# A two-block transformer kernel on one core: the first filter tap of a short convolution, the order of weight splits and four DMA issues change engines or places

## The reference, cut to what matters

```python
# even layer: bias of each head by distance, projections, compression of keys and values
hp @ w_in                      # q, k, v and the rest, one product
silu(blocks @ w1) @ w2         # blocks of 32 rows, for keys and for values
table[:, rel_bucket(dist)]     # added to the scores of 16 heads
# mixer: projection, causal depthwise convolution with 4 taps, silu
proj = h @ w_in
xbc = silu(causal_depthwise_conv(xbc, conv_w, conv_b))   # 1536 channels, out[t] = b + sum_w conv_w[w] * u[t - 3 + w]
```

## Time and profile before

| what | value |
|---|---|
| median of 3 runs | 1286.62 us (1284.84 to 1290.71) |
| the profiled execution's own time | 1286.62 us |
| its span, first to last instruction | 1284.8 us |
| TensorE busy | 95% |
| VectorE, ScalarE, GpSimd busy | 65%, 51%, 18% |
| mean granted TensorE clock | 0.982 |

### The profile page before, as it was taken

The page is one execution under the profiler, slowest core; times in us unless marked ns, Lnnn a source line. Parts: engine busy times, 40 slices in busy tenths (PEclk is TensorE's granted clock), DMA queues, the critical chain, the costliest instruction groups (busy, mean ns, idle before and its releaser), DMA issues.

```text
span 1284.8 us, 19110 instructions
## 1 busy us (share of the span) xinstructions
PE 1223.2 (95%) x7700; PEld 1058.4 (82%) x7700; DVE 839.2 (65%) x1308; ACT 656.0 (51%) x1076; POOL 230.9 (18%) x284
## 2 busy tenths in 40 slices
PE   7897899999999889999999999999999889999996
PEld 6785588888888568888888889999996579888996
DVE  6955586665586467666657776467766756766743
ACT  6425566644333556664446555446635444655531
POOL 4003431110000332121112221000005201112101
PEclk9999999999999999999999999999999879999999
DMA  7790155564454324555544554543440024455461
GB/s 275 269 200 14 54 197 171 190 222 174 163 197 155 141 99 173 188 196 194 184 182 162 196 198 153 197 175 141 162 185 1 1 77 162 164 196 175 155 206 56
DMA packets 34088, 205.56 MB, mean 160 GB/s; under 512 B 3776, under 2 KB 6352, under 8 KB 13776
## 3 DMA queue, kind: packets, MB, share of 16 engines
q1 hardware_dynamic: 30704, 200.47, 44.0%
q10 hardware_dynamic: 3296, 3.87, 1.6%
HBM read 202.87 MB, written 1.46 MB: 159 GB/s over the span
## 4 chain that ended last, share of the span: by engine, by line
PE 79%; DVE 14%; ACT 3%; POOL 1%; issue 1%; DMA 0%; POOLq 0%; ACTq 0%; DVEq 0%
PE ps L660 35%; PE ps L665 23%; PE ps L663 5%; PE ps L664 5%; DVE wl L602 4%; PE ps L684 1%; PE ps L686 1%; PE ps L685 1%; DVE tf L2173 1%; POOL pb L992 1%; PE ps L907 1%; PE ps L973 1%; ACT wh L573 1%; DVE y L1960 1%; DVE xb L738 1%
## 5 line engine op out<-in xcount | busy, mean ns | idle before, releaser
L602 DVE TENSOR_TENSOR wl<-raw,wh 128x2048 fp32r<-128x2048 f32 (+4 forms) x196 | 421.2, 2154 | 150.6 <-ACT wh L573 150.4
L660 PE MATMUL ps<-xb,wh 128*128 128x512 f32 x1424 | 502.3, 398 | 4.4 <-DVE wl L602 3.9
L665 PE MATMUL ps<-xb,wl 128*128 128x256 f32 x1696 | 476.2, 281 | 0.0
L573 ACT ACTIVATE wh<-raw 128x2048 fp32r<-128x2048 f32 (+4 forms) x196 | 348.6, 1781 | 157.9 <-PE ps L665 123.6
L660 PEld LDWEIGHTS ps<-xb,wh 128*128 128x128 f32 x1424 | 267.4, 188 | 71.1 <-issue 5.6
L665 PEld LDWEIGHTS ps<-xb,wl 128*128 128x128 f32 x1696 | 321.5, 190 | 0.0
L665 PE MATMUL ps<-ab,wl 128*128 128x256 f32 x1088 | 307.2, 282 | 0.0
L660 PE MATMUL ps<-ab,wh 128*128 128x512 f32 x640 | 226.8, 399 | 0.8 <-DVE ab L1002 0.8
L665 PEld LDWEIGHTS ps<-ab,wl 128*128 128x128 f32 x1088 | 207.0, 190 | 0.0
L660 PEld LDWEIGHTS ps<-ab,wh 128*128 128x128 f32 x640 | 120.2, 188 | 31.7 <-DVE ab L1002 1.4
L857 DVE TENSOR_TENSOR tf<-ps,tf 128x256 f32<-128x256 f32 x148 | 61.9, 421 | 119.3 <-ACT tf L852 119.3
(11 more groups left out here) (326 smaller groups left out, 1372.1 us busy)
## 6 DMA issues: line engine op xcount, KB each, us to landing
raw<-wstream SPq DMA_DIRECT2D x156, 1024.0 KB, 4.8
raw<-wstream SPq DMA_DIRECT2D x32, 704.0 KB, 4.1
raw<-wstream SPq DMA_DIRECT2D x8, 768.0 KB, 4.2
e_bt<-scratch ACTq DMA_DIRECT2D x16, 128.0 KB, 9.7
o_bt<-scratch SPq DMA_DIRECT2D x2, 1024.0 KB, 10.2
raw<-wstream SPq DMA_DIRECT2D x2, 560.0 KB, 10.1
raw<-wstream SPq DMA_DIRECT2D x4, 256.0 KB, 6.4
h<-xt ACTq DMA_DIRECT2D x4, 256.0 KB, 7.5
```

The lines of the kernel that those rows point to most:

```text
L573: e.g.activation(WH[i % HLN][:, 0:w], RAW[i % RAWN][:, 0:w], ACT.Copy).then_inc(S["hi"], 1)
L602: e.g.tensor_tensor(WL[q][:, 0:w], RAW[i % RAWN][:, 0:w], f32(WH[q][:, 0:w]), ALU.subtract).then_inc(S["lo"], 1)
L660: e.g.matmul(PS[b][:, :].rearrange("p (a t) -> p a t", a=2), wh[:, sl], x2[:, :, cs], start=start, stop=k == p.nk - 1, skip_group_check=pair)
L665: ins = e.g.matmul(o, wl[:, sl], xh[:, cs], start=False, stop=k == p.nk - 1, skip_group_check=pair)
```

## The change

1. The convolution's tap 1 moves from VectorE to GpSimd: for each of 12 tiles one multiply into the upper half of `tf` and one add to ScalarE's result. VectorE keeps taps 2 and 3, and waits for GpSimd. The lags go: VectorE does pair p-1 behind evicting pair p, ScalarE applies the silu of pair p-1 ahead of tap 0 of pair p.
2. `behind_norm`, `next_low`, `tight` and the early low part of u4 go: low parts follow the plain rule of `dve_gemm`, and so does the high part of u5; `mz` is taken with `behind` 1 instead of 0.
3. The low parts of `cmpk` and `cmpv` ahead of and inside `km` go, and follow the plain rule.
4. The scratch write and both spreads go from ScalarE's queue to SyncE's, between the weight fetches; the load of `vecs` goes from the head of ScalarE's queue to the second place of SyncE's.

```diff
-        def dve_gemm(e, p, behind, after=None, drain=None, ahead=2, first=None, between=None, tight=0):
+        def dve_gemm(e, p, behind, after=None, drain=None, ahead=2, first=None, between=None):
...
-                        lo_to(e, i + 2 - tight)
+                        lo_to(e, i + 2)
...
                 e.g.dma_start(RAW[0][:, s], w0[:, s]).then_inc(S[f"q{i}"], 16)
+                if i == 0:
+                    e.g.dma_start(V[:, :], vdram).then_inc(S["d_v"], 16)
...
         def act_begin(e):
-            e.g.dma_start(V[:, :], vdram).then_inc(S["d_v"], 16)
...
             sp_gemm(e, G["km"])
-            for name in ("cmpk", "cmpv", "qn", "ks", "ev0"):
+            e.wait_ge(S["row"], 1)
+            row = TMP[1][0:16, 0:384]
+            e.g.dma_start(bass.AP(scratch.tensor, 0, [[16 * 385, 16], [385, 16], [1, 384]]),
+                          bass.AP(row.tensor, row.offset, [list(row.ap[0]), [0, 16], [1, 384]])).then_inc(S["d_scr"], 16)
+            for name in ("cmpk", "cmpv", "qn"):
                 sp_gemm(e, G[name])
+            spread_bias(e, 1)
+            sp_gemm(e, G["ks"])
+            sp_gemm(e, G["ev0"])
+            spread_bias(e, 0)
...
-            lo_to(e, G["cmpk"].first + 1)
-            dve_gemm(e, G["km"], 1, drain=dve_to(G["km"], e_km, 0), between=lambda e, c: lo_to(e, G["cmpv"].first))
+            dve_gemm(e, G["km"], 1, drain=dve_to(G["km"], e_km, 0))
...
+            def drain_u(e, pair):
+                if pair:
+                    silu_u(pair - 1)
+                e.wait(G["mu"].out[pair])
+                e.wait_ge(S["zero"], 3)
+                for f in (2 * pair, 2 * pair + 1):
+                    e.g.activation(TF[f % 4][:, 0:T], uv[:, f, 0:T], ACT.Identity, scale=v_("convw", 4 * f, 1),
+                                   bias=v_("convb", f, 1)).then_inc(S["cva"], 1)
...
-            act_gemm(e, G["mu"], after=behind_norm, drain=drain_u)
+            act_gemm(e, G["mu"], after=act_finish(5, 1e-6), drain=drain_u)
...
         def pool_mixer(e):
+            for pair in range(6):
+                for f in (2 * pair, 2 * pair + 1):
+                    c, d = TF[f % 4][:, 0:T], TF[f % 4][:, T:2 * T]
+                    e.wait(G["mu"].out[pair])
+                    e.wait_ge(S["zero"], 3)
+                    if f >= 4:
+                        e.wait_ge(S["cts"], f - 4 + 1)
+                    e.link(e.g.tensor_scalar(d, uv[:, f, 1:1 + T], v_("convw", 4 * f + 1, 1), 0.0, ALU.mult, ALU.add))
+                    e.settle()
+                    e.wait_ge(S["cva"], f + 1)
+                    e.g.tensor_tensor(c, c, d, ALU.add).then_inc(S["cvp"], 1)
...
-                    e.wait_ge(S["cva"], f + 1)
-                    for w in (1, 2, 3):
+                    e.wait_ge(S["cvp"], f + 1)
+                    for w in (2, 3):
...
-                if pair == 0:
-                    lo_to(e, p.first + 4)
-                if pair >= 2:
-                    taps_u(pair - 2)
+                if pair:
+                    taps_u(pair - 1)
...
-                if pair < 2:
-                    taps_u(4 + pair)
-
-            def next_low(e, c):
-                if c > 2:
-                    lo_to(e, G["mu"].first + c + 2)
-
-            dve_gemm(e, G["mu"], 1, after=dve_finish(5, 1e-6, then=scaled(32.0 ** -0.5)), drain=drain_u, between=next_low,
-                     tight=1)
-            dve_gemm(e, G["mz"], 0, drain=drain_z)
+                if pair == 0:
+                    taps_u(5)
+
+            dve_gemm(e, G["mu"], 1, after=dve_finish(5, 1e-6, then=scaled(32.0 ** -0.5)), drain=drain_u)
+            dve_gemm(e, G["mz"], 1, drain=drain_z)
```

More of the change, by code:

```diff
@@ L371, in stream_no @@
     return 1 + at // 4 if c == 0 else 5 + at // 8 if c == 1 else 5 + c
-SEMS = ("er ct0 ct1 gated iv ptd rl eps psa psb pss pr ysq ysum acc adt ah al blk blkh blkl bt0 bt1 const cq cts cum cva cvd cz d_c d_out d_scr d_v ea "
+SEMS = ("er ct0 ct1 gated iv ptd rl eps psa psb pss pr ysq ysum acc adt ah al blk blkh blkl bt0 bt1 const cq cts cum cva cvd cvp cz d_c d_out d_scr d_v ea "
         "ev_act ev_dve rel low ex fah fal gemm gp gq gs gz h_down0 h_down1 h_eo h_oo hi lam_a lam_d lf lo mh ml mx na "
@@ L1142, in act_even @@
                 e.g.activation(e_blkh[:, sl], blk[i][:, 0:480], ACT.Copy).then_inc(S["blkh"], 1)
[L1143 to L1146, removed]
             act_gemm(e, G["km"])
@@ L1155, in act_even @@
             act_gemm(e, G["qn"])
-            spread_bias(e, 1)
             act_gemm(e, G["ks"])
-            spread_bias(e, 0)
             act_gemm(e, G["ev0"], drain=act_toks(G["ev0"], e_v, 0, 0))
@@ L2053, in silu_u @@
                     e.g.activation(uv[:, f, 3:259], TF[f % 4][:, 0:T], ACT.Silu).then_inc(S["cts"], 1)
[L2055 to L2071, removed]
+            def drain_u(e, pair):
[6 more added lines that the diff above has]
+                                   bias=v_("convb", f, 1)).then_inc(S["cva"], 1)
             def drain_z(e, pair):
-                if pair < 3:
-                    drain_u(e, 6 + pair)
+                if pair == 0:
+                    silu_u(5)
                 zs = m_zs[:, pair * 512:pair * 512 + 512]
@@ L2170, in taps_u @@
                     c = TF[f % 4][:, 0:T]
-                    e.wait_ge(S["cva"], f + 1)
-                    for w in (1, 2, 3):
+                    e.wait_ge(S["cvp"], f + 1)
+                    for w in (2, 3):
                         ins = e.g.scalar_tensor_tensor(out=c, in0=uv[:, f, w:w + T], scalar=v_("convw", 4 * f + w, 1), in1=c,
                                                        op0=ALU.mult, op1=ALU.add)
-                        if w < 3:
+                        if w == 2:
                             e.link(ins)
```

## The result

| | before | changed |
|---|---|---|
| median of 7 runs each | 1287.83 us (1284.84 to 1290.71) | 1299.47 us (1293.99 to 1306.98) |
| the profiled execution's own time | 1286.62 us | 1302.14 us |
| its span | 1284.8 us | 1300.3 us |
| mean granted TensorE clock | 0.982 | 0.977 |

The ratio is 1.0113, with a 95% interval of 1.0090 to 1.0137; that is 11.6 to 17.6 us. The medians lie 11.6 us apart, the two profiled executions 15.5 us. With the others on record there are 24 executions of the changed kernel: one disturbed one (1513.77 us at a mean granted clock of 0.743) is left out, and the median of the other 23 is 1302.14 us. The forecast was +8.0 us, 1294.6 us, so its side was right and its size too small. The median of the seven lies just inside the stated range of 1287.5 to 1300 us, the profiled execution and the median of the 23 lie above it.

What follows compares the result with a forecast made beforehand. The prediction took TensorE, busy 95% of the span, as the bound, so gaps ahead of matmuls count. Mixer 6.4, even-layer splits 0.6, spread 1.0 and vectors 0 sum to +8.0 us: 1294.6 us, 8-in-10 range 1287.5 to 1300.

Steps and rivals of the forecast that it cites:

- stall ahead of u5: Mixer's start: u5's low part comes behind three pairs' taps, so TensorE starts u5 5.9 us late.
- clock behind it: Mixer, behind u5's stall: TensorE runs at 1.2 GHz instead of 2.4 for a while, +1.6 us.
- given back at q0 and q1: Mixer: the delay fills TensorE's idle 0.83 us ahead of q1 and about 0.3 ahead of q0, -1.1 us.
- even-layer splits and scratch write: Even layer's start: reordered low parts make chunk 9 0.6 us late; the scratch write delays chunk 7's fetch 1.1 us, costing nothing.
- the spread: Even layer: half the bias ahead of chunk 13's fetch delays the drain of ks some 2 us; +1.0, from 0 to +4.
- vectors: Kernel's start: vecs on SyncE's queue is the same bytes ahead of the same instruction; 0, from -0.7 to +0.8 us.
- The ring: Mixer's convolution: each pair passes VectorE's taps, ScalarE's silu and tap 0, GpSimd's multiply and add; 4.21 us a pair.
- rival (c): Mixer: GpSimd is held by VectorE's taps, 0.95 us more for each of three pairs, +2.9, 1297.5 us; chance 0.13.
- rival (d): Even layer: chunk 13 so late that TensorE waits 4 us ahead of ev0; +5 instead of +1, 1298.6 us; chance 0.12.
- a sign of being wrong: Even layer: the prediction called itself wrong if ev0 started over 4 us late; it expected 1 to 2 us.
- (a): Mixer: tap 0, silu and GpSimd always keep ahead of VectorE; mixer +0.3 us, whole +1.9, 1288.5 us; chance 0.15.
- (b): Mixer: VectorE's lighter round removes TensorE's idle times ahead of u5, q0 and q1; 1284.5 us; chance 0.05.

Runs made afterwards that it cites:

- e1: Kernel before with only the even layer's part: vectors' load, scratch write and spreads on SyncE's queue, low parts by the plain rule; 1293.07 us, ratio 1.0047.
- e12: Changed kernel with 52 extra matmuls, whose results nobody reads, ahead of u5; 1299.33 us, ratio 1.0102 to before.
- e10: Kernel before with the whole new mixer (short lags, new split order), but tap 1 on VectorE; 1296.03 us in one run.
- e4: Kernel before with only both spreads of the bias moved to SyncE's queue; 1290.70 us, ratio 1.0026.
- e13: As e4, but chunk 13's fetch goes ahead of the first half of the spread on SyncE's queue; 1285.31 us in one run.
- e5: Kernel before with only the scratch write moved, ahead of chunk 7's fetch on SyncE's queue; 1295.22 us in one run.
- e7: Kernel before with e5's scratch write and e6's low parts together; 1288.79 us in one run.
- e6: Kernel before with only the low parts of cmpk and cmpv around km put on the plain rule; 1285.31 us in one run.
- e11: Kernel before with only tap 1 moved to GpSimd, old lags and split order kept; 1288.66 us, ratio 0.9992.
- e3: Kernel before with only the load of vecs moved to the second place of SyncE's queue; ratio 0.9994.
- e9: Kernel before with only the new convolution in the mixer (GpSimd's tap, short lags), old split order kept; 1303.58 us in one run.
- e15: Kernel before with tap 1 on GpSimd at the old lags and u4's low part ahead of the norm; 1289.34 us, ratio 1.0003.

## Why the prediction was wrong, by its own steps

| term of the sum | forecast, us | measured, us |
|---|---|---|
| stall ahead of u5 | 5.9 | 7.1 |
| clock behind it | 1.6 | 1.95 |
| given back at q0 and q1 | -1.1 | -0.7 |
| the mixer | +6.4 | +8.35 |
| even-layer splits and scratch write | 0.6 + 0 | 2.6 (same code in e1, e12: 1.1, 1.0) |
| the spread | 1.0 | 2.4 + 1.5 behind it (e1, e12: 5.0, 4.9) |
| vectors | 0 | 1.35 (e1, e12: 0.95, 1.2) |
| sum | +8.0 | +16.2 |

Between `ev0` and u4 0.3 us are given back, which makes the 15.9 at q1; 15.5 are left at the end.

**The mixer: the mechanism held, its size was short.** The ring gates, GpSimd and ScalarE stand between VectorE's pieces, there is one stall, its clock loss follows and q1 gives 1.0 us back. The ring was put at 4.21 us and takes 4.6. In it the term that was mis-sized is the taps'. The forecast took them at 0.48 us each and let the ring close over the second tile's; in the chain it closes over all four, 0.70 + 1.48 + 0.50 us with a hop. The source views of the taps, changed kernel and kernel before (ns, min/median/max):

```profile
L2177 DVE SCALAR_TENSOR_TENSOR tf<-m_u,vecs,tf x24: 474/655/846, 892.0 to 922.1; 128x256 f32<-128x256 f32 x24
```

```profile
L2173 DVE SCALAR_TENSOR_TENSOR tf<-m_u,vecs,tf x36: 473/485/486, 886.2 to 917.0; 128x256 f32<-128x256 f32 x36
```

and of GpSimd's add in the changed kernel:

```profile
L2140 POOL TENSOR_TENSOR tf<-tf x12: 725/774/1708, 891.2 to 920.1; 128x256 f32<-128x256 f32 x12
```

Four taps take 2.7 us for a pair now, where the forecast had 1.9. In e10, with the same lags and without GpSimd, a tap takes 484 ns in the median and 486 at most, so it is GpSimd beside them that makes them longer. GpSimd's add keeps its 0.77 us beside them and has 1.7 only beside a low part. So rival (c) was right that sharing costs time and wrong about who pays: not GpSimd, held for 0.95 us in each of three pairs, but VectorE. The ring grew by 0.4 us, which is 0.7 over the two rings behind pair 0; pair 0's own round took 0.6 more. So u5 is 1.2 us later than forecast, not 2.9. The rule of the Trainium skill, "GPSIMD Engine Reference", section "Specifications", that GpSimd contends with VectorE instructions with two SBUF inputs, agrees with these rows; the prediction held against it and looked only at GpSimd's side. The same group shows VectorE's: two of L738 in 1.43 us beside GpSimd, 0.72 each, and a tap of that kind takes 0.48.

**The spread: the step that failed most.** The prediction put chunk 13 near 73 us, its low part's end near 77 and the drain of `ks` some 2 us later. On before's clock (3.97 us taken off) the copy starts at 74.0, the low part ends at 78.2 and the drain comes 3.5 us later. It then priced the drain's delay at 1.0, half of it, by the small products of the compression. They hide only 1.2 us: TensorE waits 2.2 us (+2.4 on the lateness), and the stretch at the low clock behind it takes 1.5 more (1.7 in e4, 2.5 in e1 and e12); 4.0 us alone in e4. That is rival (d), which had 0.12, and `ev0` starts 6.4 us late, past the 4 us that the prediction named as a sign of being wrong. The row that decides was there: the earlier trace rows has 10.2 us for a megabyte in rows of 1 KB, the half that now goes first. "The same bytes cross the same engines now" was the wrong reason against (d). Before, chunk 13 is fetched 4 us ahead of that traffic, and it is chunk 15 that takes 12.3 us to land, with time to spare; in the changed kernel chunk 13 is fetched behind it. e13 moves only that and the loss is gone.

The Trainium skill, "DMA: Bandwidth & Descriptors", section "Issuing engines are not separate DMA queues", says that DMAs run on the same 16 engines and interleave, whichever engine starts them. These traces agree: e13 issues the same spreads from SyncE without loss, and the 12.3 us of chunk 15 in before come with the spreads on ScalarE's queue.

**The scratch write: "nothing is lost" was wrong.** The fetch of chunk 7 goes out at 38.39 as forecast, but the copy can only start at 48.16, 9.8 us on, against the 4.8 of the earlier trace rows; the 384 KB ahead of it cost it 5 us of landing on top of the 1.1 us of issue. By itself this costs 3.0 us (e5), with the new splits 0.8 to 1.1 us (e7, e1, e12), and 2.6 in the changed kernel's own trace. The splits' own +0.6 was near (e6, +0.4), though the prediction's terms 43.9 + 4.8 + 1.9 give 50.6 and not the 51.1 that it wrote; but the idle times ahead of chunks 7, 8 and 9, which were to take up their delay, were now used up by the late landings.

**The vectors: outside the bounds.** The bytes are the same, but `vecs` lands at 8.6 us in the second place of SyncE's queue, where the prediction had 7.26 and at most +0.8. The first matmul is 1.35 us late.

**The rivals.** (a), that the ring doesn't gate, and (b), faster, fell: the first stall is 7.40 us. The result lies at the range's upper end and, by the profiled execution, above it; that it isn't further off is owed to (d)'s price, which set that end. (d) and a larger ring were treated as alternatives, of which one comes; they are independent, and both came.

**What stays open.** The landing of chunk 8 named above, and that the loss behind the wait ahead of `ev0` is the clock's. The medians of seven are 11.6 us apart where the profiled executions and the lateness have 15.5; the median of 23 executions of the changed kernel is 14.3 us above before's, and the interval of the ratio takes all of these in.

## What to carry to other kernels

A lag in a software pipeline across engines is worth more than the work it moves. With the lag of two pairs tap 1 could run on either engine at no price; without it every pair pays the whole round trip, whoever does the tap. Of a DMA that is moved, ask which transfers go out behind it, on any queue, and what it takes to land, not what it takes to issue; a fetch that must be on time goes ahead of anything in small rows. And a short wait of TensorE in a stretch of small products can cost about twice its length (2.1 us became 4.0 in e4). And where single parts are worth less than the whole time's scatter, compare the starts of the same matmuls in two traces.

## What the runs showed of the hardware that was not expected

- VectorE's three-operand instruction of 128x256 goes from 485 to 655 ns in the median (up to 846) beside GpSimd's tensor work; GpSimd's add goes from 0.74 to 0.77 us only, its multiply from 0.48 to 0.65. Beside a low part (VectorE's subtraction of 128x2048, which keeps its 2.28 us but for one of 2.83 in e11) it is GpSimd that takes longer: its add 1.70 us, and its multiply up to 2.77 in e11.
- The clock fell behind a wait of 2.1 us ahead of `ev0` (e4: 0.55 in the window behind it, after 4 us with 10 small matmuls), not only behind one of 7.4 us. Before's idle times of 0.29 and 0.83 us ahead of u5 and q1, between full products, have 1.00 in their windows.
- The matmul stream has two paces at a granted clock of 1.00: in the wide products 150 matmuls take either 26.38 or 25.88 us from the first start to the last, 1.9% apart, and an execution keeps one pace for a whole product. From 228 us on, before has 26.38 and e3, e4 and e10 have 25.88; from 733 us on before has 25.88, and e4, e9, e10, e11 and e15 26.38. It is worth up to 3 us in a product. What sets it wasn't found.
- More of the scatter lies between 1000 and 1060 us of before's time, behind all that the change touches, where the granted clock goes down and up several times. From trace to trace the lateness changes there by -0.6 us (e3) to +4.9 us (e5), with 24 to 41 us at the low clock; it is +1.4 in the changed kernel and +4.1 in e1. The windows of before and of e5 over about the same stretch (before starts 145 matmuls in 40 us, e5 107):

```profile
1010.00:1050.00 40.00, 33.31 (x145) 22.62 (x144) 27.16 (x72) 16.80 (x51) 7.30 (x9) 0.67 0.06 20
...
1014.00:1054.00 40.00, 33.74 (x107) 20.84 (x105) 26.66 (x71) 16.43 (x51) 7.31 (x9) 0.51 0.00 1
```

  This and the two paces are part of why the runs of one kernel lie between 1281.20 and 1297.11 us, and why a part's cost is read here from its own stretch.
